# Input projection of a hybrid attention and state-space layer by one level of Strassen's algorithm, in three passes over the tokens

## The reference, cut to what matters

```python
h = rmsnorm(x, norm_w)
q, k, v, z_a, xbc, z_b, dt_raw, g_a, g_b = jnp.split(h @ w_in, split_points(SPLITS), axis=-1)
# w_in: 1024 x 7184: q 1024, k 256, v 256, z_a 1024, xbc 1536, z_b 1024, dt 16, g_a 1024, g_b 1024
q = rmsnorm(q by heads, q_norm_w); k = rmsnorm(k by heads, k_norm_w)
attn = sink_attention over windows of two chunks of 64
xbc = silu(causal_conv(xbc padded with 3 earlier rows, conv_w, conv_b))      # 4 taps
y = ssd_scan(x, dt, a, b, c, h0) + d_skip * x, gated by silu(z_b), rmsnorm
x = x + (sigmoid(g_a) * ((attn * silu(z_a)) @ w_o_attn) + sigmoid(g_b) * (y @ w_o_ssd)) @ w_out
```

## Time and profile before

| | |
|---|---|
| median of 3 runs | 2425.28 us |
| the profiled execution | 2424.73 us |
| its span | 2422.7 us |
| PE matmul busy | 2284.8 us (94%), 12671 matmuls |
| PE weight load busy | 2060.7 us (85%), 12671 loads |
| DVE busy | 808.8 us (33%) |
| ACT busy | 831.4 us (34%) |
| POOL busy | 617.4 us (25%) |
| HBM traffic over the span | 158.48 MB read, 90.81 MB written |

### The profile page before, as it was taken

One profiled execution on the slowest core, in us unless ns is written; L12 is line 12 of the kernel. 1 busy time (PEld: TensorE's weight loads), 2 busy tenths in 40 slices (PEclk: granted clock), 3 DMA queues, 4 the chain that ended last, 5 costly groups with the idle time before them and its releaser, 6 DMA issues. The chain is left out here.

```text
span 2422.7 us, 35225 instructions
## 1 busy us (share of the span) xinstructions
PE 2284.8 (94%) x12671; PEld 2060.7 (85%) x12671; DVE 808.8 (33%) x1504; ACT 831.4 (34%) x1925; POOL 617.4 (25%) x539
## 2 busy tenths in 40 slices
PE   6999999999999999999999859999956999996999
PEld 5999999999999999999999848888744878874887
DVE  4211100004444100100000056555517899983221
ACT  5211111124444211221111155555526666742010
POOL 3101010110111110101101045555514777760000
PEclk9999999999999999999999979999987999998999
DMA  4411111112112112121121965444436777735333
GB/s 158 97 72 54 72 70 72 53 71 88 53 71 77 64 71 80 62 80 54 71 88 53 79 157 122 115 104 105 106 93 189 193 196 199 200 107 174 130 130 100
DMA packets 273859, 250.09 MB, mean 103 GB/s; under 512 B 75208, under 2 KB 250168, under 8 KB 266616
## 3 DMA queue, kind: packets, MB, share of 16 engines
q1 hardware_dynamic: 269592, 248.78, 35.9%
q10 hardware_dynamic: 4208, 0.54, 0.2%
HBM read 158.48 MB, written 90.81 MB: 103 GB/s over the span
## 5 line engine op out<-in xcount | busy, mean ns | idle before, releaser
L74 PE MATMUL acc<-h_hi,w_hi 128*128 128x424 f32 (+1 forms) x2280 | 810.8, 356 | 10.2 <-DVE h_lo L561 7.8
L75 PE MATMUL acc<-h_lo,w_hi 128*128 128x424 f32 (+1 forms) x2280 | 807.9, 354 | 0.0
L76 PE MATMUL acc<-h_hi,w_lo 128*128 128x424 f32 (+1 forms) x2280 | 807.8, 354 | 0.0
L74 PEld LDWEIGHTS acc<-h_hi,w_hi 128*128 128x128 f32 x2280 | 430.2, 189 | 24.7 <-DVE h_lo L561 8.6
L75 PEld LDWEIGHTS acc<-h_lo,w_hi 128*128 128x128 f32 x2280 | 430.8, 189 | 7.3
L76 PEld LDWEIGHTS acc<-h_hi,w_lo 128*128 128x128 f32 x2280 | 430.7, 189 | 7.4
L332 POOL TENSOR_TENSOR w_lo<-w_raw,w_hi 128x1024 fp32r<-128x1024 f32 x57 | 144.7, 2539 | 1130.7 <-ACT w_hi L374 1130.7
L399 ACT ACTIVATE row<-acc 128x424 f32<-128x424 f32 (+1 forms) x215 | 112.7, 524 | 825.5 <-PE acc L76 825.4
L597 DVE SCALAR_TENSOR_TENSOR conv_acc<-conv_in,conv_wb,conv_acc 128x424 f32<-128x424 f32 (+2 forms) x216 | 126.1, 584 | 380.9 <-ACT conv_acc L444 373.1
L74 PE MATMUL a_o_ps<-a_w_hi,a_at_hi 128*128 128x512 f32 (+1 forms) x272 | 117.1, 430 | 2.0 <-DVE a_branch L1292 2.0
L1120 ACT ACTIVATE a_prob<-a_score,a_neg_max 128x129 f32<-128x129 f32 x264 | 103.3, 398 | 44.9 <-DVE a_neg_max L1259 42.2
(11 more groups left out here) (215 smaller groups left out, 3016.3 us busy)
## 6 DMA issues: line engine op xcount, KB each, us to landing
proj<-row SPq DMA_DIRECT2D x56, 1056.0 KB, 4.0
w_raw<-in_w_in_dram SPq DMA_DIRECT2D x28, 1024.0 KB, 5.2
s_feat<-proj SPq DMA_DIRECT2D x16, 1280.0 KB, 8.8
s_acs_b<-acs_dram SPq DMA_DIRECT2D x16, 1024.0 KB, 8.2
a_q_diag<-proj SPq DMA_DIRECT2D x66, 128.0 KB, 4.3
a_z<-proj SPq DMA_DIRECT2D x16, 512.0 KB, 4.8
a_gate_t<-proj SPq DMA_DIRECT2D x16, 512.0 KB, 4.6
branch_rows<-a_branch SPq DMA_DIRECT2D x16, 512.0 KB, 3.2
```

Source lines behind the costliest of these rows:

```text
L74: pe.matmul(out, hi, whi, start=first, stop=False)
L75: pe.matmul(out, hi, wlo, start=False, stop=False)
L76: return pe.matmul(out, lo, whi, start=False, stop=last)
```

## The change

`project_inputs` is rewritten. The 2112 tokens are handled in three passes of 704, each as two sides of 352. For each pass, h is kept transposed and unsplit in four quarters, h11, h12 (first 512 features) and h21, h22 (last 512 features) by left and right side. Three sums replace parts of them, and seven right operands of 512 x 352 are split into `hh` (ACT) and `hl` (DVE). The 56 weight tiles (dt is taken out) are handled as 28 pairs. For each pair, SP loads 1024 x 256 weights, DVE forms three sums and one change in place (`weight_sums`), ACT makes seven high parts and POOL seven low parts of 512 elements a partition. PE makes seven products of 4 x 3 matmuls of 352 columns, in the order 0, 1, 3, 2, 6, 5, 4. Some products add onto a bank that ACT has first copied to `part` (`copy_part`); DVE adds banks and copies to the four results (`total_of`, `finish_pair`). The banks x and z and the copies are there twice, by even and odd pairs. The weights are loaded and split again in each pass.

Row functions (silu, sigmoid) run on ACT from SBUF (`pre` to `row`), one pair late; the convolution runs on whole rows of 704 with the taps one pair late and silu two pairs late, and its three last inputs are carried over to the next pass. In the order of pairs, the six convolution pairs stand at places 6, 8, ..., 16 of a pass, with silu pairs between them. The blocks of x of the next pass (88 rows each) are prepared in pairs 6, 8, ..., 20 of a pass. dt is computed by PE from the unsplit h with 16 columns of weights (`dt_products`), its softplus stands in pair 5 of the last pass, the tail stores at pair 19 of the last pass. All loops on the engines are written out.

```diff
-        h_hi = sb("h_hi", [P, KT, TOK], F32R)
-        h_lo = sb("h_lo", [P, KT, TOK], F32R)
+        PASSES, NB, XR = 3, 352, 88
+        PW = 2 * NB
+        PAIR_COUNT = 28
+        PRODUCTS = 7
+        hh = sb("hh", [P, PRODUCTS, 4, NB], F32R)
+        hl = sb("hl", [P, PRODUCTS, 4, NB], F32R)
+        hraw = sb("hraw", [P, 4, 4, NB])
+        w_raw = sb("w_raw", [P, 2, KT, 2 * P])
+        part = sb("part", [P, 2, 4, NB])
+        x_ps = pb("x_ps", [P, 2, BANK])
+        z_ps = pb("z_ps", [P, 2, BANK])
+        RIGHT = [h11, h21, t2, h11, h12, t3, h22]
+        ORDER = [0, 1, 3, 2, 6, 5, 4]
+        PREP = [6, 8, 10, 12, 14, 16, 18, 20]
+        COLUMN_PAIRS = [0, 1, 2, 3, 4, 5, 10, 6, 11, 7, 12, 8, 13, 9, 14, 16, 15, 17, 18, 19, *range(20, PAIR_COUNT)]
...
         @block.sync
+            for n in range(ALL):
+                p, i = divmod(n, PAIR_COUNT)
+                if n + 2 < ALL:
+                    load_raw(n + 2)
+                if n + 2 < ALL and prepared(n + 2) is not None:
+                    load_x(prepared(n + 2))
+                if n and kind_at(n - 1) != "conv":
+                    store(n - 1)
...
+                if p == PASSES - 1 and i == 19:
+                    sp.wait_ge(carried, 2 * CONV_PAIRS * PASSES)
...                 # the six stores of the tail rows
         @block.gpsimd
+            def split_lo(n, j):
+                pool.wait_ge(whi_ready, products_to(n, j))
+                pool.tensor_tensor(wl[:, j], left(n, j), wh[:, j].bitcast(FP32), ALU.subtract).then_inc(wlo_ready, 1)
+            for n in range(ALL):
+                for j in ORDER:
+                    if n + 1 < ALL:
+                        split_lo(n + 1, j)
+                    if j == 1 and prepared(n) is not None:
+                        rstd(prepared(n))
         @block.scalar
+            def split_hi(n, j):
...
+                after(act, product_done, products_to(n - 1, j) if n else 0)
+                act.activation(wh[:, j], left(n, j), ACT.Copy).then_inc(whi_ready, 1)
+            def h_high(p, j):
...
+                act.activation(hh[:, j], RIGHT[j], ACT.Copy).then_inc(hhi_ready, 1)
+            def copy_part(n, k):
+                j, bank = [(0, x_bank(n)), (3, z_bank(n)), (2, x_bank(n)), (4, x_bank(n))][k]
+                act.wait_ge(product_done, products_to(n, j))
+                after(act, summed, 4 * (n - 2) + [1, 3, 2, 4][k])
+                act.activation(part_of(n, k), bank[:, 0:NB], ACT.Copy).then_inc(part_copied, 1)
         @block.vector
+            def weight_sums(n):
+                a11, a12, a21, a22 = a[:, 0:4, 0:P], a[:, 4:8, 0:P], a[:, 0:4, P:2 * P], a[:, 4:8, P:2 * P]
+                dve.wait_ge(raw_loaded[n % 2], 16 * (n // 2 + 1))
+                after(dve, wlo_ready, products_to(n - 1, 5) if n else 0)
+                dve.tensor_tensor(ws[:, 1], a11, a21, ALU.subtract).then_inc(s_ready, 1)
+                dve.tensor_tensor(a21, a21, a22, ALU.add).then_inc(s_ready, 1)
+                dve.tensor_tensor(ws[:, 0], a21, a11, ALU.subtract).then_inc(s_ready, 1)
+                dve.tensor_tensor(ws[:, 2], a12, ws[:, 0], ALU.subtract).then_inc(s_ready, 1)
+            def h_low(p, j):
+                dve.wait_ge(hhi_ready, products_to(p, j))
+                dve.tensor_tensor(hl[:, j], RIGHT[j], hh[:, j].bitcast(FP32), ALU.subtract).then_inc(hlo_ready, 1)
+            def total_of(n, f, side, bank, k, j):
+                dve.wait_ge(product_done, products_to(n, j))
+                dve.wait_ge(part_copied, 4 * n + k + 1)
+                for to, a, b in sum_target(n, f, side):
+                    ins = dve.tensor_tensor(to, bank[:, a:b], other[:, a:b], ALU.add)
+            def finish_pair(n):
+                dve.wait_ge(part_copied, 4 * n + 4)
+                dve.tensor_tensor(p4, u4, p4, ALU.subtract).then_inc(u_minus_p, 1)
+                total_of(n, 1, 1, z_bank(n), 1, 5)
+                total_of(n, 0, 1, r_ps, 3, 6)
+            for n in range(ALL):
+                if n:
+                    finish_pair(n - 1)
...
+                if n + 1 < ALL:
+                    weight_sums(n + 1)
...
+                total_of(n, 0, 0, q_ps, 0, 1)
+                if kind_at(n - 1) == "conv":
+                    taps(n - 1, 1)
+                if n and prepared(n - 1) is not None:
+                    weigh(prepared(n - 1))
+                if kind_at(n - 1) == "conv":
+                    taps(n - 1, 0)
...
+                if prepared(n) is not None:
+                    normalise(prepared(n))
+                total_of(n, 1, 0, z_bank(n), 2, 5)
         @block.tensor
+            def product(n, j):
+                x, z = x_bank(n), z_bank(n)
+                bank, first = [(x, True), (q_ps, True), (x, False), (z, True), (x, False), (z, False), (r_ps, True)][j]
+                pe.wait_ge(wlo_ready, products_to(n, j))
...
+                if j in (2, 4, 5):
+                    pe.wait_ge(part_copied, 4 * n + {2: 1, 5: 2, 4: 3}[j])
+                if j == 6:
+                    after(pe, summed, 4 * (n - 1) + 4)
...
+                for k in range(4):
+                    pe.matmul(out, wh[:, j, k], hh[:, j, k], start=first and k == 0, stop=False, skip_group_check=more)
+                    pe.matmul(out, wh[:, j, k], hl[:, j, k], start=False, stop=False, skip_group_check=more)
+                    mm = pe.matmul(out, wl[:, j, k], hh[:, j, k], start=False, stop=k == 3, skip_group_check=more)
+                mm.then_inc(product_done, 1)
```

More of the change, by code:

```diff
@@ L117, in project_inputs @@
+        r_ps = pb("r_ps", [P, BANK])
         xt = pb("xt", [P, 2, BANK])
[L119 to L141, removed]
+        qs = xt
+        xflat = xbuf[:, :, :].rearrange("p a n -> p (a n)")
@@ L189, in rows_of @@
[L189 to L212, removed]
+        zeroed = sem("zeroed")
@@ new lines, in project_inputs, with kind_of @@
+        Q_PAIRS, CONV_FIRST, CONV_PAIRS = 4, 6, 6
+        PREP = [6, 8, 10, 12, 14, 16, 18, 20]
+        DT_PAIR = 22
+        LAST = PAIR_COUNT - 1
+        ORDER = [0, 1, 3, 2, 6, 5, 4]
+        PLACE = [ORDER.index(j) for j in range(PRODUCTS)]
+        COLUMN_PAIRS = [0, 1, 2, 3, 4, 5, 10, 6, 11, 7, 12, 8, 13, 9, 14, 16, 15, 17, 18, 19, *range(20, PAIR_COUNT)]
+        FUNC = {"silu": ACT.Silu, "sigmoid": ACT.Sigmoid}
+        def kind_of(i):
+            o = COLUMN_PAIRS[i]
+            if o < Q_PAIRS:
+                return "query"
+            if o < 6:
+                return "copy"
+            if o < 10 or 16 <= o < 20:
+                return "silu"
+            return "conv" if o < 16 else "sigmoid"
@@ L474, in _ @@
-            evacuate_first(0, UNITS - 1)
-            split_hi(2, 0, 0, 2)
-            evacuate_first(1, UNITS - 2)
-            evacuate_first(1, UNITS - 1)
-            act.wait_ge(params, 16 * (2 * TAPS))
-            act.wait_ge(hist_zero, 1)
-            for first, last, kind in segments():
-                with act.Fori(max(first, 1), min(last, pairs - 1)) as p:
-                    for s in range(2):
-                        T = 2 * p + s
-                        split = (T + 1, 1 - s, 1 - s, p + 1 + s)
-                        if kind == "conv":
-                            conv_tile(T, s, p, split)
-                        else:
-                            plain_tile(T, s, p, ACT.Silu if kind == "silu" else ACT.Copy, split, kind == "query")
@@ new lines, in last_conv, with hist_to, conv_silu @@
+            def last_conv(n):
+                return max(m for m in range(n) if kind_at(m) == "conv")
+            def hist_to(n, f):
+                p = n // PAIR_COUNT
+                done = 2 * (conv_index(n) - CONV_PAIRS * p) + 2 - f
+                return done if p == 1 else 2 * CONV_PAIRS + 2 * done
+            def conv_silu(n, f):
+                p = n // PAIR_COUNT
+                act.wait_ge(taps_ready, taps_before(n, f, len(tap_pieces(p))))
+                after(act, stored[n % 2], 16 * (n // 2))
+                act.activation(row[:, n % 2, f, :], conv_acc[:, f, :], ACT.Silu).then_inc(row_ready, 1)
@@ L541, in _ @@
-            plain_tile(NT - 2, 1, NT // 2 - 1, ACT.Sigmoid, (NT - 1, 0, 1, pairs + 1 + NG // 2))
-            plain_tile(NT - 1, 0, NT // 2, ACT.Sigmoid, None)
+            square(0)
+            square(1)
+            act.wait_ge(rel_mm, 1)
+            act.activation(onehot[0:NH, :], q_ps[0:NH, 0:NREL], ACT.Copy).then_inc(rel_copied, 1)
+            for g in range(2, XT):
+                square(g)
+                if g == 5:
+                    split_hi(0, 0)
+                    split_hi(0, 1)
+                    split_hi(0, 3)
@@ L544, in _ @@
+            finish_pair(ALL - 1)
+            function_row(ALL - 1, 1)
+            function_row(ALL - 1, 0)
         @block.vector
         def _(dve):
[L546 to L554 removed]
```

1003 lines of the change are left out of this document (584 added, 419 removed).

## The result

The changed kernel takes 2413.79 us (median of 5 runs, 2409.77 to 2415.33) against 2425.28 (5 runs, 2424.45 to 2427.75): ratio 0.9948, 95% interval 0.9934 to 0.9963. Faster, by 0.5%. I had forecast 2323 with a range down from 2395: the sign was right, the size a ninth of what I wrote (11.5 us against 102), and the time lies outside the range.

What follows compares the result with a forecast made beforehand. It took PE alone to bound the input projection; start 44, products 1130, other PE work 25, port 50, turns 16, then 5, 5 and 4 summed to 1279 against 1381.4 us, giving 2323 us, range 2258 to 2395.

Steps and rivals of the forecast that it cites:

- Products: PE's 7056 matmuls of 352 columns in the input projection, at 160.2 ns each: 1130 us.
- The rivals that touch the interval (0.147, 0.188): Matmul interval: 147 ns if the 13.5 ns addition vanishes (2270 us, chance 0.04); 188 if weight loads bound (chance 0.08).
- Start, end, other PE work: Effective start before steady pairs 44 us; stage's end +4; transposes, query sums, dt products and tables on PE 25.
- DVE and POOL exclude each other: Shared port in convolution pairs: PE waits 3.6 us per two pairs, 50 us in all (bounds 10 and 85).
- the query pairs: Pairs with the queries' extra square (1.6 us): taken as hidden; softplus chain and query squares 5 us together (0 to 14).
- Tail stores: Six 3-row stores at pair 19 of the last pass hold SP's queue and delay ACT's load: 5 us (0 to 12).
- Turns: Changes of pass, where seven high and low parts are remade: 8 us each, two turns 16 (bounds 4 to 30).
- Waits drop the clock: Rival: waits in each pair of pairs drop PE to 1.2 GHz, 18 x 3 = 54 us more, 2377; chance 0.20.
- The weight-load rival: Rival: loads must end before matmuls start, interval 188 ns, products 1327 us, port waits 5 and 4, total 2454; chance 0.08.
- full blocking: Convolution-pair port term if the lock held for the whole instruction, with no start hidden: about 82 us.

Runs made afterwards that it cites:

- freeing the port: Changed kernel with POOL's low parts of all weights but the first pair's left out (4 elements a partition instead of 512): 2283.9 us, ratio to before 0.9408.
- experiment 10: Changed kernel with the normalise of the 16 inner x blocks still on DVE, as a product of two inputs instead of the scalar form: 2421.2 us.
- 12: Changed kernel with POOL clearing one element a partition after each low part in the 16 pairs with a normalise of x: 2418.4 us.
- order only: Changed kernel with normalise of inner x blocks and query squares moved to ACT and tail stores spread, low parts staying on POOL: 2327.0 us.

## Why the prediction was wrong

- **Products**: right. 0.160 us at 352 columns, 1129 us against 1130. The rivals that touch the interval (0.147, 0.188) are out.
- **Start, end, other PE work**: right within 5 us each (47.2 against 44; the end +4.1 against +4; about 29 against 25). For the start this is luck in part: I had the first product near 34 and the first pair slowed by 9 us; it came at 42.9, and the pair was only 4.3 us over.
- **DVE and POOL exclude each other**: the mechanism was right; freeing the port brings 131 us. Its size in the convolution pairs was too small: 80.6 - 10.5 = 70 us against 50, inside the bounds of 10 and 85. Some 13 of the 70 are the lower clock, which I had left to a rival. And the place was right in part only: I had PE wait behind the taps; in the first two passes the 12 long gaps of these pairs, 3.1 to 3.7 us each, stand ahead of the transposes of x, for a normalise that I had priced at 0.69 us and that took 8.0; behind the taps stand four, of 1.7 to 1.8.
- **The failed step** is the query pairs: "hidden, with the queries' extra square just over", and "the softplus chain and the query squares I take at 5 together". Measured: 38.7 + 6.3 = 45. I compared the sum of work in a pair with the pair's length. But PE asks for the squares behind its fourth product, 7.7 us into the pair, and they stood behind a subtraction, two totals and four weight sums. Two of the sums and the square itself each let a POOL low part in ahead, and the square ended 9.9 us into the pair. The second experiment moved only the square's place, and the loss went.
- **Tail stores**: 18.4 against 5, above my bound of 12. I had the queue's hold but let the load behind it land in its usual time; it took 17 us.
- **Turns**: 21.6 against 16, inside the bounds of 4 to 30.
- **Waits drop the clock**, the rival of 0.20: it happens, but costs 30 us in all, and 13 in the pairs for which I had 54. By the rows, intervals behind the wait at 545 are at 0.29 us. In the kernels whose waits are gone it is 4 to 5.

- **Two figures beside the sum** don't follow from its terms. The weight-load rival is 2323 + 197 - 45 - 12 = 2463, not 2454. And no working leads to the 82 us of full blocking: the demand of 31.7 against 27.8, counted as the 50 was (x 18, less 15), gives 55.

The sum of the misses, 40 + 20 + 13 + 6 + 3 + 4 = 86 us, takes 1279 to 1365; the stage's end counted as I did (1374.19 - 8.5) is 1365.7. Some 5 us more went behind the stage, which I had left as it is: from PE's first work of the next to the last matmul it is 1033.7 us against 1028.3. All twelve variants of the changed kernel have 1031 to 1035 there too; why is open.

The Trainium skill (SBUF: State Buffer, Who interferes with whom) gives the port as a lock held for a whole instruction, and by full blocking I had put the convolution term at 82. The measured 70, 57 without the clock, lies between that and my 50. The section has whoever issues first take the port and the other wait until it is through. The waiting agrees with the trace. The order does not settle it: the normalise, begun at 654.41, was passed by five low parts whose rows begin later (655.61 and on).

## What to carry to other kernels

Where two engines share a port, adding up work per period says whether it fits, not whether it is in time: for each point at which the bounding engine asks for a result, add up what stands ahead of it in that engine's order, each with one operation of the other engine, and know that it can be more (six, ahead of the normalise here). Move such operands early, or to an engine that doesn't take the port; here it was best to give all the low parts to the engine that is faster at them (0.69 us against 1.29). And a transfer behind stores of tiny pieces (here six of 6 KB in packets of 4 bytes) can be late by more than the time that the queue is held.

## What the runs showed of the hardware that I had not expected

- DVE operations on the port let at most one POOL low part end before theirs, with one exception: of 574 others without an input in PSUM in the changed kernel (60 to 1250 us, copies left out) 306 saw one end inside and 268 none. The normalise saw two (4 times) or six (12). Its form is not the reason (experiment 10), a short POOL operation in between doesn't let it in (12). In "order only" the subtraction of `finish_pair` had the same 12 times, four low parts, 4.54 us for 0.51. What decides stays open.
- The lower clock level comes behind gaps of 2.2 us already, for 5 to 18 intervals (0.7 to 2.4 us), but not behind every one: of the gaps of 3.23 us in the changed kernel some have 11 or 12 such intervals behind them and some none.
- The addition to columns over 2.4 GHz is 13.3 ns at 352 columns, as at 416 and 512: a third width.
